# A triangular inverse built from blocks of 4 with half-width merges, and weight sums formed by an accumulating DMA

## The chip, the cores and the metric

The kernel runs on one core of one Trainium2 chip. The metric is the device time of one execution in microseconds; the time before is the median of three runs. A trace of one further execution shows what each engine did. The engines are named as the profile names them: PE (TensorE), PEld (its weight loads), DVE (VectorE), ACT (ScalarE), POOL (GpSimd), SP (the queue that issues most transfers).

## What is computed

One layer of a hybrid decoder over 512 tokens of width 2048, all in float32. The cut reference:

```python
h = rms_norm(x, norm_w)
proj = h @ w_in            # two branches (8 heads of 128 each), their gates
# branch A, per head, chunks of 64 tokens:
a_mat = where(strict, beta * (k @ k.T) * exp(cum_g[i] - cum_g[j]), 0)
sol   = triangular_solve(eye + a_mat, [v * beta, k * beta * exp(cum_g)], lower, unit_diagonal)
# ... chunk-by-chunk state recurrence with qk, q_dec, k_dec, g_last
# branch B, per head: block-sparse softmax attention (blocks of 256 keys)
y_gdn, y_moba = oa @ w_out_gdn, ob @ w_out_moba
merged = sigmoid(g_gdn) * y_gdn + sigmoid(g_moba) * y_moba
x = x + merged @ w_o
```

The triangular solve is done here through the explicit inverse of `eye + a_mat`, a 128x128 matrix for each of four groups of 128 tokens.

## The kernel before

**The head loop.** Eight heads follow one another, 117.7 us each. PE works through the input projection in windows: `win(n, k0, k1)` is the k steps k0 to k1 of a window, three 128x512 matmuls each (lines 740, 742, 744), and between these pieces stand the small products of branch A of head h and of branch B of head h-1. Every engine's program is written out by hand in one fixed order and paced by counted semaphores, so each small product stands some k steps behind the one whose result it needs. `four(ps, lhsT, rhs)` (L769) is four 128x128 products for the four token groups; the trace shows eight matmul instructions for it, each with its own weight load. `turn(ps, src)` (L774) is four transposes, four instructions.

**The inverse.** DVE forms the exponent of the decay matrix with one instruction for each token group (L1692), ACT takes the exponential, POOL masks it (L644). `kk` multiplies the products of the keys by it, `UT` and `LT` turn the result twice. From the blocks of 16 on the diagonal (`Ud`, `Ld`), `n1` to `n4` build the inverse of these blocks by repeated squaring. `ma(h, k)` and `mb(h, k)` then merge blocks: ma takes the product of the masked lower part with the inverse so far, and the inverse's transpose; mb multiplies the two and DVE adds the result. Levels 0 and 1 (to blocks of 32 and 64) work on full 128x128 matrices, level 2 on 64x64 corners. `vTs` turns v, and DVE scales it to `vb`, which ma(h, 0) waits for.

**The quads.** After the heads come ten quads 0 to 9 with 224 units of 12 matmuls (L1161, L1163, L1165), 2.74 us a unit when nothing waits. A quad multiplies four blocks of weights in seven products, named P11, PS1, PS2, P12, PS4, PS3, P22. ACT copies a unit's operand to `ring_hi` (L1520, `op_hi`), DVE forms `ring_lo` (L2117, `op_lo`), and PE uses both. Quads 0 to 3, 8 and 9 have four units a product; quads 4 to 7 have two (their weights are w_out_gdn and w_out_moba). PS1 takes the weights A21 - A11 and PS2 that sum plus A22. With four units POOL adds A22 by an accumulating DMA on the operand in place (`add_22`, L691), issued when op_lo has read PS1's operand. With two units DVE does it (`form_t2`, L2219), from a copy of A22 in the upper half of slot A. POOL's queue also stores the blocks (`finish_block`, L699, L702) and in quads 6 and 7 accumulates them from memory (L710).

ACT's order around a product is: `op_hi` of PS2's two units, then the copies of P11's result out of PSUM (L1561, `copy_out`), which PE waits for before it writes the same banks for PS2.

**The last head** has no next projection, and DVE puts ten `own_step` instructions (L2077, 128x2048) between its other work.

Of the kernel before, what the change touches and what calls it, by code (L numbers as in the profile page):

```python
# [13 lines left out]
P = 128  # L14
# [66 lines left out]
def t_base(q):  # L81
    return sum((3 if ku(b) == 4 else 4) * ku(b) for b in range(q))
# [6 lines left out]
def t2_formed(q, j):  # L89
    return t_base(q) + ku(q) + j + 1  # L90


def t4_formed(q, j):
    return t_base(q) + (1 if ku(q) == 4 else 2) * ku(q) + j + 1


def t3_formed(q, j):
    return t_base(q) + (2 if ku(q) == 4 else 3) * ku(q) + j + 1


def added(q):
    return 16 * (sum(ku(b) == 4 for b in range(q)) + 1)
# [20 lines left out]
def place(n):  # L123
# [41 lines left out]

(HC_G, HC_CG, HC_B, HC_NB, HC_NBE, HC_KD, HC_GL) = range(7)
# [11 lines left out]
 hcol cgrow_mm cg_rows cg_arg cg_eg cg_dt cg_dts  # L178
 conv clampd sig silu sqd sq_hi sq_lo ss_mm rn_ln rn norm
 kT_mm kdec kk_mm kkd qk_mm qkd qdec UT_mm Ln LT_mm Ud Ld X1 L32m L64m  # L180
 n1_mm L2 U2 n2_mm X2 L4 U4 n3_mm X4 L8 n4_mm X8 ma_mm Y XT mb_mm X
# [10 lines left out]
def hybrid_layer(nc, x, norm_w, w_in, gdn_conv_w, gdn_a_log, gdn_dt_bias, gdn_norm_w, moba_q_norm_w,  # L192
# [8 lines left out]
    cg_dram = nc.dram_tensor("decay_rows", (H, T), F32, kind="Internal").ap()  # L201
# [5 lines left out]
    with ctx:  # L207
# [41 lines left out]
        cg_rows = sg[:NT * H, 0, 1, 0:P]  # L249
# [29 lines left out]
        lm = [sb(f"lower{i}", [P, T], at=area) for i in range(3)]  # L279
# [27 lines left out]
        cgb = sb("decay_row", [P, T], at=area)  # L307
# [8 lines left out]
        Eg, L2, Yt = w2_, w2_, w2_  # L316
        dTs, L4 = w0_, w0_
        Up, U2, XTt = w1_, w1_, w1_
        Ud, U4, vn = w3_, w3_, w3_
        Ld, L8, o1 = w4_, w4_, w4_  # L320
        Ln = lm[0]
# [7 lines left out]
        def tile4h(t):  # L329
            return slice(t * P, t * P + P // 2), slice(t * P + P // 2, (t + 1) * P)  # L330

# [284 lines left out]
        def _(pool):  # L616
# [15 lines left out]
            def decay_row(h):  # L632

                pool.wait_ge(s["cg_eg"], h)
                pool.wait_ge(s["cg_arg"], 4 * h)
                pool.dma_start(cgb[:], cg_dram[bass.ds(h, 1), :].broadcast_to([P, T])).then_inc(s["cg_rows"], 16)

            def head(h, p):
# [3 lines left out]
                pool.wait_ge(s["cg_dt"], h + 1)  # L642
                pool.wait_ge(s["n3_mm"], h)
                pool.tensor_tensor(q4(dTs), q4(dT), over(plane(C_STRICT)), ALU.mult).then_inc(s["cg_dts"], 1)  # L644
# [7 lines left out]
                pool.wait_ge(s["Ln"], h + 1)  # L652
                pool.wait_ge(s["ma_mm"], 3 * h)
                pool.tensor_tensor(q4(lm[1]), q4(Ln), over(plane(C_L32)), ALU.mult).then_inc(s["L32m"], 1)
                pool.tensor_tensor(q4(lm[2]), q4(Ln), over(plane(C_L64)), ALU.mult).then_inc(s["L64m"], 1)
# [19 lines left out]
            pool.wait_ge(s["hc_set"], 2 + NHC + 1)  # L675
            for t in range(NT):
                pool.dma_start(cg_dram[:, tile4(t)], cg_rows[t * H:(t + 1) * H, :]).then_inc(s["cg_rows"], 16)
# [38 lines left out]
            for q in range(NQ):  # L716
                if q == W0:
                    finish_block(q - 1, 3)
                if ku(q) == 4:
                    add_22(q, 0)  # L720
                    add_22(q, 1)
                if q > 0 and q != W0:
                    finish_block(q - 1, 3)
                if ku(q) == 4:
                    add_22(q, 2)
                    add_22(q, 3)
                for i in range(3):
                    finish_block(q, i)
# [6 lines left out]
        def _(pe):  # L735
# [42 lines left out]
            def cgrow(h):  # L778
                pe.wait_ge(s["hcol"], h + 1)
                for t in range(NT):  # L780
                    mm = pe.matmul(G2[:, tile4(t)], hcol[:, HC_G, t:t + 1].broadcast_to([P, P]), triu,
                                   start=True, stop=True)
                mm.then_inc(s["cgrow_mm"], 1)
# [23 lines left out]
            def UT(h):  # L807
                pe.wait_ge(s["kkd"], h + 1)
                pe.wait_ge(s["kdec"], h + 1)
                turn(G0, Up).then_inc(s["UT_mm"], 1)  # L810

            def LT(h):
                pe.wait_ge(s["Ln"], h + 1)
                turn(G2, Ln).then_inc(s["LT_mm"], 1)

            def n1(h):
                pe.wait_ge(s["Ud"], h + 1)
                pe.wait_ge(s["Ld"], h + 1)
                pe.wait_ge(s["qkd"], h + 1)
                four(G0, Ud, Ld)  # L820
                four(G1, Ld, Ud).then_inc(s["n1_mm"], 1)

            def n2(h):
                pe.wait_ge(s["L2"], h + 1)
                pe.wait_ge(s["U2"], h + 1)
                pe.wait_ge(s["X1"], h + 1)
                four(G0, U2, L2)
                four(G1, L2, U2)
                four(G2, L2, xa).then_inc(s["n2_mm"], 1)

            def n3(h):
                pe.wait_ge(s["X2"], h + 1)
                pe.wait_ge(s["L4"], h + 1)
                pe.wait_ge(s["U4"], h + 1)
                four(G0, U4, L4)
                four(G2, L4, xb).then_inc(s["n3_mm"], 1)

            def n4(h):
                pe.wait_ge(s["X4"], h + 1)
                pe.wait_ge(s["L8"], h + 1)  # L840
                four(G2, L8, xa).then_inc(s["n4_mm"], 1)

            def vTs(h):
                pe.wait_ge(s["silu"], 3 * h + 3)
                pe.wait_ge(s["U4"], h + 1)
                turn(G1, cv["gv"]).then_inc(s["vT_mm"], 1)

            def ma(h, k):
                src = (xb, xa, xb)[k]
                if k == 0:  # L850
                    pe.wait_ge(s["X8"], h + 1)
                    pe.wait_ge(s["L8"], h + 1)
                    pe.wait_ge(s["vb"], h + 1)
                elif k == 1:
                    pe.wait_ge(s["X"], 3 * h + k)
                if k < 2:
                    pe.wait_ge((s["L32m"], s["L64m"])[k], h + 1)
                    four(G0, lm[k + 1], src)
                    mm = turn(G1, src)
                else:  # L860
                    for t in range(NT):
                        a, b = tile4h(t)
                        pe.matmul(G0[:P // 2, b], Ln[P // 2:, a], src[P // 2:, b], start=True, stop=True)
                    for t in range(NT):
                        a, b = tile4h(t)
                        mm = pe.transpose(G1[:P // 2, a], src[:P // 2, a], ident[:P // 2, :P // 2])
                mm.then_inc(s["ma_mm"], 1)

            def mb(h, k):
                if k < 2:  # L870
                    pe.wait_ge(s["Y"], 3 * h + k + 1)
                    pe.wait_ge(s["XT"], 3 * h + k + 1)
                    mm = four(G2, XTt, Yt)
                else:
                    for t in range(NT):
                        a, b = tile4h(t)
                        mm = pe.matmul(G2[:P // 2, b], XTt[:P // 2, a], Yt[:P // 2, b], start=True, stop=True)
# [8 lines left out]
            def vnew(h, t):  # L886
                if t == 0:
                    pe.wait_ge(s["vb"], h + 1)
                    pe.wait_ge(s["X"], 3 * h + 3)
                else:  # L890
                    pe.wait_ge(s["vbk"], 3 * h + t)
                pe.matmul(G1[:, :P], xb[:, tile4(t)], vb[:, tile4(t)], start=True, stop=True).then_inc(s["vn_mm"], 1)
# [57 lines left out]
            def head(h, p):  # L950
# [21 lines left out]
                else:  # L972
# [6 lines left out]
                    pe.transpose(A2[:NT * H, P:2 * P], ba[:, 1].rearrange("p t h -> p (t h)"), ident[:])\  # L979
# [7 lines left out]
                UT(h)  # L987
                win(2, 12, 14)
                ss(h, 1)
                win(2, 14, 15)  # L990
                LT(h)
                win(2, 15, 16)
                win(3, 0, 1)
                qk(h)
                win(3, 1, 4)
                n1(h)
                win(3, 4, 7)
                n2(h)
                win(3, 7, 10)
                n3(h)  # L1000
                win(3, 10, 13)
                n4(h)
                win(3, 13, 16)
                vTs(h)
                win(4, 0, 2)
# [1347 lines left out]
```

## Time and profile before

| what | value |
|---|---|
| median of 3 runs | 1641.9 us (1641.84, 1641.90, 1643.56) |
| the profiled execution, its own time | 1643.3 us |
| its span, first to last instruction | 1641.8 us |
| PE busy | 1592.5 us (97%), 7858 matmul instructions |
| PEld busy | 1316.3 us (80%) |
| DVE busy | 1092.7 us (67%) |
| ACT busy | 790.1 us (48%) |
| POOL busy | 158.3 us (10%) |
| granted PE clock, share of full | 0.994 |

The times of the rows are in us from the span's start. A busy PE is not a PE at its peak: matmuls overlap, so what an instruction costs is read from the distance between starts, not from its own length.

### The profile page before, as it was taken

The numbers are of one execution on the slowest core, as the hardware profiler recorded it, in microseconds if no ns is written. First come the engines' busy times: TensorE is split into PE (matmuls) and PEld (weight loads), VectorE is DVE, ScalarE is ACT, GpSimd is POOL, SyncE is SP. The second block draws the span as 40 slices with busy tenths as digits, with TensorE's granted clock in tenths as the row PEclk, the third lists the DMA queues.
The fourth block names the chain that finished last, engine by engine and source line by source line (L and its number), as shares of the span: only waits on it lengthen the run. The fifth ranks groups of instructions, "written<-read, shape, count | busy, mean of one in ns | idle before, by whom it ended". The sixth has DMA issues, their size and how long they took to land.

```text
span 1641.8 us, 20823 instructions
## 1 busy us (share of the span) xinstructions
PE 1592.5 (97%) x7858; PEld 1316.3 (80%) x7858; DVE 1092.7 (67%) x1320; ACT 790.1 (48%) x1048; POOL 158.3 (10%) x154
## 2 busy tenths in 40 slices
PE   6999999999999999999999999999999999999997
PEld 5888888887887887887887887888888778777885
DVE  5745745645646646556568758867677999888863
ACT  5434534435434444335335346556465845447442
POOL 4101001001001000010011011011010000001011
PEclk9999999999999999999999999999999999999999
DMA  8304314223223233133143337576566556775653
GB/s 261 78 26 115 84 38 129 57 76 90 77 57 99 73 77 96 51 89 83 51 113 101 137 136 210 192 192 220 140 189 187 196 196 209 202 217 112 196 116 52
DMA packets 192379, 206.19 MB, mean 126 GB/s; under 512 B 7491, under 2 KB 139846, under 8 KB 190726
## 3 DMA queue, kind: packets, MB, share of 16 engines
q1 hardware_dynamic: 176470, 161.69, 33.2%
q0 software_dynamic: 15856, 43.80, 11.2%
q8 instruction: 33, 0.54, 0.1%
q14 instruction: 20, 0.16, 0.0%
HBM read 180.28 MB, written 29.38 MB: 128 GB/s over the span
## 4 chain that ended last, share of the span: by engine, by line
PE 81%; issue 6%; DVE 5%; DMA 5%; ACT 2%; POOL 1%; SPq 0%; ACTq 0%; POOLq 0%; DVEq 0%
PE bank L740 14%; PE bank L744 14%; PE bank L742 14%; PE bank L1161 8%; PE bank L1163 8%; PE bank L1165 8%; PE bank L769 6%; DMA e_block<-branch_a 2%; PE bank L774 1%; DVE ring_lo L2117 1%; PE bank L930 1%; PE bank L946 1%; DMA operands<-branch_a 1%; ACT ring_hi L1520 1%; PE bank L940 1%
## 5 line engine op out<-in xcount | busy, mean ns | idle before, releaser
L740 PE MATMUL bank<-h_hi_r,w_hi 128*128 128x512 f32 x1008 | 421.5, 418 | 0.0
L744 PE MATMUL bank<-h_hi_r,w_raw_r 128*128 128x512 f32 x1008 | 396.9, 394 | 0.0
L742 PE MATMUL bank<-h_lo_r,w_hi 128*128 128x512 f32 x1008 | 394.1, 391 | 0.0
L2117 DVE TENSOR_TENSOR ring_lo<-operands,ring_hi 128x1024 fp32r<-128x1024 f32 x224 | 271.8, 1221 | 117.8 <-ACT ring_hi L1520 116.8
L1520 ACT ACTIVATE ring_hi<-operands 128x1024 fp32r<-128x1024 f32 x224 | 235.5, 1059 | 230.0 <-PE bank L1165 174.4
L744 PEld LDWEIGHTS bank<-h_hi_r,w_raw_r 128*128 128x128 f32 x1008 | 189.1, 188 | 43.0
L742 PEld LDWEIGHTS bank<-h_lo_r,w_hi 128*128 128x128 f32 x1008 | 190.3, 189 | 35.6 <-issue 1.7
L740 PEld LDWEIGHTS bank<-h_hi_r,w_hi 128*128 128x128 f32 x1008 | 189.9, 188 | 35.8 <-issue 1.7
L1161 PE MATMUL bank<-ring_hi,h_hi_r 128*128 128x512 f32 x480 | 190.6, 397 | 3.1 <-issue 3.1
L1163 PE MATMUL bank<-ring_lo,h_hi_r 128*128 128x512 f32 x480 | 189.4, 395 | 0.0
L1674 DVE TENSOR_TENSOR w_raw_r<-w_raw,w_hi 128x2048 fp32r<-128x2048 f32 x64 | 146.7, 2292 | 45.9 <-ACT w_hi L1219 44.7
L1165 PE MATMUL bank<-ring_hi,h_lo_r 128*128 128x512 f32 x416 | 162.4, 390 | 0.0
L1165 PE MATMUL bank<-ring_hi,sums_r 128*128 128x512 f32 x384 | 150.1, 391 | 0.0
L1161 PE MATMUL bank<-ring_hi,sums_r 128*128 128x512 f32 x320 | 126.3, 395 | 7.6 <-DVE ring_lo L2117 4.3
L1163 PE MATMUL bank<-ring_lo,sums_r 128*128 128x512 f32 x320 | 125.1, 391 | 0.0
L1219 ACT ACTIVATE w_hi<-w_raw 128x2048 fp32r<-128x2048 f32 x64 | 122.2, 1909 | 0.0
L1161 PEld LDWEIGHTS bank<-ring_hi,h_hi_r 128*128 128x128 f32 x480 | 90.4, 188 | 24.5 <-issue 4.1
L1163 PEld LDWEIGHTS bank<-ring_lo,h_hi_r 128*128 128x128 f32 x480 | 90.7, 189 | 18.5 <-issue 0.2
L1165 PEld LDWEIGHTS bank<-ring_hi,h_lo_r 128*128 128x128 f32 x416 | 78.4, 188 | 17.3
L1165 PEld LDWEIGHTS bank<-ring_hi,sums_r 128*128 128x128 f32 x384 | 72.5, 189 | 15.6
L1161 PEld LDWEIGHTS bank<-ring_hi,sums_r 128*128 128x128 f32 x320 | 60.4, 189 | 22.5 <-issue 7.2
L1163 PEld LDWEIGHTS bank<-ring_lo,sums_r 128*128 128x128 f32 x320 | 60.5, 189 | 12.3
(324 smaller groups left out, 2179.4 us busy)
## 6 DMA issues: line engine op xcount, KB each, us to landing
w_raw<-in_w_in_dram SPq DMA_DIRECT2D x64, 1024.0 KB, 6.0
operands<-in_w_in_dram SPq DMA_DIRECT2D x64, 512.0 KB, 4.7
operands<-in_w_o_dram SPq DMA_DIRECT2D x32, 512.0 KB, 4.9
operands<-in_w_in_dram POOLq DMA_DIRECT2D x16, 512.0 KB, 8.7
gates<-e_block POOLq DMA_DIRECT2D x16, 512.0 KB, 5.3
operands<-in_w_out_gdn_dram SPq DMA_DIRECT2D x16, 512.0 KB, 4.0
operands<-gates SPq DMA_DIRECT2D x16, 512.0 KB, 5.2
operands<-in_w_out_moba_dram SPq DMA_DIRECT2D x16, 512.0 KB, 4.6
```

What stands on the lines that cost most here:

```text
L740: pe.matmul(PJ[slot % 2][:], w_hi[slot % 2][:, c], h_hi[:, k, :], start=(k == 0), stop=False, skip_group_check=True)
L742: pe.matmul(PJ[slot % 2][:], w_hi[slot % 2][:, c], h_lo[:, k, :], start=False, stop=False, skip_group_check=True)
L744: mm = pe.matmul(PJ[slot % 2][:], w_lo[slot][:, c], h_hi[:, k, :], start=False, stop=(k == KT - 1), skip_group_check=True)
L769: mm = pe.matmul(ps[:, tile4(t)], lhsT[:, tile4(t)], rhs[:, tile4(t)], start=True, stop=True)
L774: mm = pe.transpose(ps[:, tile4(t)], src[:, tile4(t)], ident[:])
L1161: pe.matmul(ps[:], a_hi, ring_hi[:, n % RINGS, c], start=(FRESH[p] and k == 0), stop=False, skip_group_check=True)
L1163: pe.matmul(ps[:], a_hi, ring_lo[:, n % RINGS, c], start=False, stop=False, skip_group_check=True)
L1165: mm = pe.matmul(ps[:], a_lo, ring_hi[:, n % RINGS, c], start=False, stop=(k == kn - 1), skip_group_check=True)
L1219: act.activation(w_hi[slot % 2][:], raw[slot][:], ACT.Copy).then_inc(s["hi_ready"], 1)
L1520: act.activation(ring_hi[:, n % RINGS, :], operand(q, p, j), ACT.Copy).then_inc(s["op_hi"], 1)
L1674: dve.tensor_tensor(w_lo[slot][:], raw[slot][:], w_hi[slot % 2][:].bitcast(F32), ALU.subtract)\
L2117: dve.tensor_tensor(ring_lo[:, n % RINGS, :], operand(q, p, j), ring_hi[:, n % RINGS, :].bitcast(F32), ALU.subtract).then_inc(s["op_lo"], 1)
```

## The change

**The inverse.** The squaring now stops at blocks of 4 (n1 and n2, one `four` each), and four levels of merges go from blocks of 4 to 64, then the unchanged level of 64x64 corners. In a merge from blocks of b only the rows and columns that change are touched: the matrix has m = 128 - b rows, and only every second block of columns moves, 64 of 128. The masked product is formed after PE, by DVE, which multiplies the 64 columns by a mask of pairs.

**Both orientations of the decay.** Instead of turning the product twice, the kernel forms the upper matrix (`dTb`) and the lower one (`dL`, `dLm`) of decay, beta and mask ahead of the product. The rows -beta are loaded beside the decay rows by the same transfer, now 128x1024. Three DVE instructions of 128x512 take the place of the four of 128x128, ACT gets a third exponential, POOL four products instead of three.

**The quads.** `form_t2` is gone; `add_22` runs for every quad.

```diff
@@ cgrow on DVE
-                for t in range(NT):
-                    dve.scalar_tensor_tensor(dT[:, tile4(t)], row[:, tile4(t)], hcol[:, HC_CG, t:t + 1],
-                                             plane(C_DMASK), ALU.subtract, ALU.add).then_inc(s["cg_arg"], 1)
+                dve.tensor_tensor(q4(dL), q4(row), hcb(HC_CG), ALU.subtract).then_inc(s["cg_arg"], 1)
+                dve.wait_ge(s["cg_arg"], 3 * h + 1)
+                dve.tensor_tensor(q4(dT), q4(dL), over(plane(C_DMASK)), ALU.add).then_inc(s["cg_arg"], 1)
+                dve.tensor_tensor(q4(dL), q4(dL), over(plane(C_CMASK)), ALU.subtract).then_inc(s["cg_arg"], 1)
@@ POOL, called at the start of each head
+            def decay_parts(h):
+                pool.wait_ge(s["cg_dl"], h + 1)
+                pool.tensor_tensor(q4(dL), q4(dL), hcb(HC_NB), ALU.mult).then_inc(s["cg_dts"], 1)
...
+                pool.tensor_tensor(q4(dTb), q4(dT), over(masked4), ALU.mult).then_inc(s["cg_dts"], 1)
...
+                pool.tensor_tensor(q4(dLm), q4(dL), over(masked4), ALU.mult).then_inc(s["cg_dts"], 1)
...
+                pool.tensor_tensor(dTb[:], dTb[:], nb_row, ALU.mult).then_inc(s["cg_dts"], 1)
@@ merges on PE
+                    m = P - b
+                    for t in range(NT):
+                        pe.matmul(G0[:m, t * PAIRED:(t + 1) * PAIRED], Ln[:, t * P:t * P + m],
+                                  half_tile(xa, t, b, 1), start=True, stop=True)
+                    for t in range(NT):
+                        mm = pe.transpose(G1[:m, t * P:t * P + m], xa[:m, t * P:t * P + m], ident[:m, :m])
...
+                    m = P - LEVELS[k]
+                    for t in range(NT):
+                        mm = pe.matmul(G2[:m, t * PAIRED:(t + 1) * PAIRED], XTt[:m, t * P:t * P + m],
+                                       Yt[:m, t * PAIRED:(t + 1) * PAIRED], start=True, stop=True)
@@ the end of the chain on PE
+                win(4, 10, 12)
                 vTs(h)
...
+                win(4, 12, 13)
+                pe.wait_ge(s["X"], NL * h + NL - 1)
+                pe.wait_ge(s["vb"], h + 1)
                 win(4, 13, 14)
+                ma(h, 4)
@@ POOL, quads
             for q in range(NQ):
...
-                if ku(q) == 4:
-                    add_22(q, 0)
-                    add_22(q, 1)
+                add_22(q, 0)
+                add_22(q, 1)
@@ DVE, quads
-            def form_t2(q, j):
...
-                dve.tensor_tensor(ops[:, SLOT_A, j, :], ops[:, SLOT_A, j, :], ops[:, SLOT_A, 2 + j, :], ALU.add)\
-                    .then_inc(s["t_formed"], 1)
```

In the first head the rows come straight from PE: `cgrow` there gets four more products (eight instructions), a second transpose and a copy, and DVE builds the masks before it (`level_masks`, nine instructions).

The order of DVE at the start of a head in the loop, before and then after. `w_raw_r` is the split of the next window's weights, `cst` holds the masks, and the rows of `bank` and `softmax_stats` are the attention of head h-1.

```order
L1674 TENSOR_TENSOR w_raw_r<-w_raw,w_hi 128x2048
L1687 ISA
L1689 REGISTER_ALU
L1692 SCALAR_TENSOR_TENSOR decayT<-decay_row,hcol,cst 128x128 x4
L1872 ISA
L1873 TENSOR_TENSOR bank<-bank,cst 128x128
```

```order
L1685 TENSOR_TENSOR w_raw_r<-w_raw,w_hi 128x2048
L1698 ISA
L1700 REGISTER_ALU
L1701 TENSOR_TENSOR lower<-decay_rows,hcol 128x512
L1702 ISA
L1703 TENSOR_TENSOR decayT<-lower,cst 128x512
L1704 TENSOR_TENSOR lower<-lower,cst 128x512
L1875 ISA
L1876 TENSOR_TENSOR bank<-bank,cst 128x128
```

Three instructions over all 512 columns now stand ahead of the first instruction of the softmax, where one group of four short ones stood.

POOL at the same place of the loop, before and then after: the last row of each is the store of branch B.

```order
L636 DMA decay_row<-decay_rows 128x512
L642 REGISTER_ALU
L644 TENSOR_TENSOR work<-decayT,cst 128x512
L649 ISA
L649 DMA branch_outputs<-probs 128x512
```

```order
L656 DMA decay_rows<-decay_rows 128x1024
L660 REGISTER_ALU
L661 TENSOR_TENSOR lower<-lower,hcol 128x512
L665 TENSOR_TENSOR work<-decayT,cst 128x512
L667 REGISTER_ALU
L668 TENSOR_TENSOR lower<-lower,cst 128x512
L670 ISA
L671 REGISTER_ALU
L672 TENSOR_TENSOR work<-work,decay_rows 128x512
L683 ISA
L683 DMA branch_outputs<-probs 128x512
```

Four products now stand together at the start of the head; the two that stood later in the head (L654, L655 of before) are gone.

POOL's queue from the end of quad 3 to quad 5, before and then after: `gates` and `branch_a` rows are stores of finished blocks, the `operands` rows that read weights are accumulating transfers.

```order
L699 DMA gates<-e_block 128x1024 x4
L702 DMA branch_a<-operands 128x1024
L702 DMA branch_a<-e_block 128x1024 x3
L702 DMA branch_a<-operands 128x1024
```

```order
L721 DMA operands<-in_w_out_gdn_dram 128x2x512 x2
L729 DMA gates<-e_block 128x1024
L732 DMA branch_a<-operands 128x1024
L732 DMA branch_a<-e_block 128x1024 x2
L721 DMA operands<-in_w_out_gdn_dram 128x2x512 x2
```

Two accumulating transfers of 512 KB now stand in each of the quads 4 to 7, ahead of the store of the last block of the quad before.

## Rows read from the trace of the kernel before

**Rows 1.** The page: busy time of each engine, its share, its instructions.

```profile
PE 1592.5 (97%) x7858; PEld 1316.3 (80%) x7858; DVE 1092.7 (67%) x1320; ACT 790.1 (48%) x1048; POOL 158.3 (10%) x154
```

**Rows 2.** Timeline of PE in the fourth head: start, length, engine, line, out<-in, shapes.

```profile
423.60 0.60 PE L774 MATMUL bank<-ident,work 128*128 128x128 f32 x4
...
424.26 0.39 PE L742 MATMUL bank<-h_lo_r,w_hi 128*128 128x512 f32 x1
424.50 0.40 PE L744 MATMUL bank<-h_hi_r,w_raw_r 128*128 128x512 f32 x1
...
428.42 1.05 PE L769 MATMUL bank<-conv_gq,conv_gk 128*128 128x128 f32 x8
...
429.55 0.40 PE L742 MATMUL bank<-h_lo_r,w_hi 128*128 128x512 f32 x1
```

**Rows 3.** Timeline of PE in the first head: weights of 128 columns, 32 moving columns.

```profile
51.21 0.30 PE L1074 MATMUL bank<-mgt,cst 128*128 128x32 f32 x2
51.35 0.39 PE L1075 MATMUL bank<-mgt,ones_f 128*128 128x32 f32 x2
...
51.89 0.39 PE L742 MATMUL bank<-h_lo_r,w_hi 128*128 128x512 f32 x1
```

**Rows 4.** Timeline of PE, the corner level mb(h, 2), weights and moving 64 wide.

```profile
464.48 0.39 PE L744 MATMUL bank<-h_hi_r,w_raw_r 128*128 128x512 f32 x1
464.80 0.68 PE L877 MATMUL bank<-work 64*64 64x64 f32 x8
...
465.75 0.39 PE L742 MATMUL bank<-h_lo_r,w_hi 128*128 128x512 f32 x1
```

**Rows 5.** Timeline of DVE at the start of the head loop's fourth head.

```profile
388.52 2.29 DVE L1674 TENSOR_TENSOR w_raw_r<-w_raw,w_hi 128x2048 fp32r<-128x2048 f32 x1 [6.18 <-ACT w_hi L1219]
390.73 1.14 DVE L1692 SCALAR_TENSOR_TENSOR decayT<-decay_row,hcol,cst 128x128 f32<-128x128 f32 x4
391.78 0.29 DVE L1873 TENSOR_TENSOR bank<-bank,cst 128x128 f32<-128x128 f32 x1
...
393.93 0.29 DVE L1886 TENSOR_SCALAR bv<-bv,softmax_stats 128x128 f32<-128x128 f32 x1
```

**Rows 6.** PE at that place, then line 940 over the span: what its waits ended on.

```profile
394.27 0.33 PE L940 MATMUL bank<-ident,bv 128*128 128x128 f32 x1
...
  DVE bv L1886: 2.9, 7
```

**Rows 7.** Timelines of POOL and of DVE where both work at once.

```profile
473.69 1.80 POOL L664 TENSOR_TENSOR k_rope<-pt,cossin 128x512 f32<-128x512 f32 x1 [46.06 <-DVE pt L1852]
...
474.37 1.67 DVE L1859 TENSOR_TENSOR pt<-pt,cossin 64x512 f32<-64x512 f32 x1
```

**Rows 8.** Timelines of PE and of DVE around the turn of v.

```profile
446.90 0.60 PE L774 MATMUL bank<-ident,conv_gv 128*128 128x128 f32 x4
...
447.54 0.69 DVE L1784 TENSOR_TENSOR v_beta<-bank,hcol 128x512 f32<-128x512 f32 x1 [1.85 <-PE bank L774]
```

**Rows 9.** Timelines of DVE and of PE in the first head.

```profile
56.79 0.18 DVE L1679 COPY hcol<-hc 128x28 f32<-128x28 f32 x1
...
57.82 1.05 PE L781 MATMUL bank<-cst,hcol 128*128 128x128 f32 x8
```

**Rows 10.** Timelines of DVE, ACT and PE in quad 4, between PS1 and PS2.

```profile
1297.95 1.21 DVE L2117 TENSOR_TENSOR ring_lo<-operands,ring_hi 128x1024 fp32r<-128x1024 f32 x1
...
1301.01 1.22 DVE L2219 TENSOR_TENSOR operands<-operands 128x1024 f32<-128x1024 f32 x1
...
1302.32 1.06 ACT L1520 ACTIVATE ring_hi<-operands 128x1024 fp32r<-128x1024 f32 x1 [4.27 <-DVE operands L2219]
...
1306.41 1.07 ACT L1561 ACTIVATE operands<-bank 128x512 f32<-128x512 f32 x2
...
1307.53 0.80 PE L1161 MATMUL bank<-ring_hi,h_lo_r 128*128 128x512 f32 x1 [3.69 <-ACT operands L1561]
```

**Rows 11.** Line 691, the accumulating transfers of before: issue to landing.

```profile
DMA to landing us min/median/max: 5.7/8.6/10.6
```

More of the change, by code:

```diff
@@ L81, in t_base, with t4_formed, added @@
 def t_base(q):
-    return sum((3 if ku(b) == 4 else 4) * ku(b) for b in range(q))
+    return sum(3 * ku(b) for b in range(q))
 def t1_formed(q, j):
     return t_base(q) + j + 1
-def t2_formed(q, j):
+def t4_formed(q, j):
     return t_base(q) + ku(q) + j + 1
-def t4_formed(q, j):
-    return t_base(q) + (1 if ku(q) == 4 else 2) * ku(q) + j + 1
 def t3_formed(q, j):
-    return t_base(q) + (2 if ku(q) == 4 else 3) * ku(q) + j + 1
-def added(q):
-    return 16 * (sum(ku(b) == 4 for b in range(q)) + 1)
+    return t_base(q) + 2 * ku(q) + j + 1
+def added(q, j):
+    return 16 * sum(j < ku(b) for b in range(q + 1))
 def op_loads(q, j, slot, nth=0):
@@ L278, in hybrid_layer @@
         w0_ = sb("work0", [P, T], at=area)
-        lm = [sb(f"lower{i}", [P, T], at=area) for i in range(3)]
+        Ln, dL, dLm = [sb(f"lower{i}", [P, T], at=area) for i in range(3)]
         xa = sb("inv_a", [P, T], at=area)
@@ L314, in hybrid_layer @@
         cos, sin = cossin[:, 0, :], cossin[:, 1, :]
[L316 to L321, printed above, removed]
+        cg_row, nb_row = rows2[:, 0, :], rows2[:, 1, :]
+        Eg, Yt = w2_, w2_
+        dTb, L2 = w0_, w0_
+        XTt = w1_
+        Ud, vn = w3_, w3_
+        Ld, o1 = w4_, w4_
+        masked4 = plane(C_STRICT)
+        steps = plane(C_L64)
         probs = [bv, pr1]
@@ L330, in tile4h, with half_of, half_tile, compact @@
             return slice(t * P, t * P + P // 2), slice(t * P + P // 2, (t + 1) * P)
+        def half_of(ap, b, which):
+            return ap[:].rearrange("p (n s b) -> p n s b", s=2, b=b)[:, :, which, :]
+        def half_tile(ap, t, b, which):
+            return ap[:, tile4(t)].rearrange("p (n s b) -> p n s b", s=2, b=b)[:, :, which, :]
+        def compact(ap, rows):
+            return ap[:rows, :NT * PAIRED]
+        def paired(k):
+            at = plane((C_M16, C_L32)[k // 2])
+            return at[:, (k % 2) * PAIRED:(k % 2 + 1) * PAIRED]
         def corner(ap, half):
@@ L782, in cgrow @@
                                    start=True, stop=True)
+                for t in range(NT):
+                    mm = pe.matmul(G1[:, tile4(t)], hcol[:, HC_NB, t:t + 1].broadcast_to([P, P]), ident[:],
+                                   start=True, stop=True)
                 mm.then_inc(s["cgrow_mm"], 1)
@@ L856, in ma @@
[L856 to L859, printed above, removed]
+                    pe.wait_ge(s["X2"], h + 1)
+                    pe.wait_ge(s["qkd"], h + 1)
+                elif k < NL - 1:
+                    pe.wait_ge(s["X"], NL * h + k)
+                if k == NL - 1:
+                    for t in range(NT):
+                        i, j = tile4h(t)
+                        pe.matmul(G0[:P // 2, j], Ln[P // 2:, i], xa[P // 2:, j], start=True, stop=True)
+                    for t in range(NT):
+                        i, j = tile4h(t)
+                        mm = pe.transpose(G1[:P // 2, i], xa[:P // 2, i], ident[:P // 2, :P // 2])
```

336 lines of the change are left out of this document (156 added, 180 removed).

## The prediction

> **What bounds the kernel now.** I first read the page's shares: PE is busy for 97% of the span and DVE for 67% [rows 1]. The span is PE's, so time taken off PE comes off the span one for one, as long as nothing that PE waits for becomes later. Then I read PE's timeline for what a group of small products costs. The lengths overlap, so I take distances between starts: from a group's first instruction to the second window product behind it, less one ordinary distance of 0.24 (424.26 to 424.50). A `four` costs 1.13 - 0.24 = 0.89 us for its eight instructions, 0.111 each; a `turn` costs 0.66 - 0.24 = 0.42 for four, 0.105 each [rows 2]. Last I looked for the places where PE does wait. In the head loop that is one, in seven heads: the first transposes of the softmax (L940) start 0.05 us after DVE has scaled `bv`, and line 940 waited 2.9 us over 7 times, so each delay of DVE there is PE's [rows 5, 6]. After the heads it is the turn from PS1 to PS2 in the two-unit quads: PE stood 3.69 us in quad 4 [rows 10].
>
> **The inverse on PE.** Before, a head has 96 instructions of `four` at full width (n1 16, n2 24, n3 16, n4 8, and 8 in each ma and mb of levels 0 and 1) and 16 transposes (UT, LT and two levels): 96 x 0.111 + 16 x 0.105 = 12.34 us. After, there are 16 for n1 and n2 (1.78), 64 in four levels of merges, and 16 transposes. The corner level and `vTs` stay. The number of groups between window pieces stays at 13, so their edges cancel.
>
> What do the 64 cost, whose weights have m = 124, 120, 112 and 96 columns (113 on average, 0.883 of 128), and whose moving side has 64? Two things could set the distance: the weight load or the moving columns. The nearest row has weights of 128 columns and only 32 moving: four instructions cost 0.68 - 0.24 = 0.44, or 0.11 each, the same as with 128 moving [rows 3]. So a narrow moving side alone gains nothing, and the weights' columns decide. I take 0.111 x 0.883: 64 x 0.098 = 6.27, and for the transposes 16 x 0.105 x 0.883 = 1.48. The sum after is 9.53, a saving of 2.81 per head, **22.5 us** for eight. Bounds: if the distance does not fall with m at all, the 80 and 16 instructions cost 10.56, and 1.78 is saved per head (14.2 in all). If the moving side counted and the 64 cost half, the sum is 1.78 + 3.55 + 1.48 = 6.81, and 5.5 is saved per head (44). The corner level speaks for some caution: with both sides at 64 its eight instructions cost 1.27 - 0.48 = 0.79, hardly less than 0.89, though the group itself is 0.68 long instead of 1.05; what is gained inside is lost at the edges [rows 4, 2]. A line between 64 and 128 columns through these totals gives 0.87 for a group of eight, and a saving of about 2.0 per head (16). I stay with 22.5, since the new groups use more than half of the array's rows and columns, as the full ones do.
>
> **The start of each head on DVE.** Behind the split of the weights the four instructions of L1692 occupy DVE for 1.05 us (390.73 to 391.78) [rows 5]. Three of 128x512 with 0.69 each [rows 8] take their place. They follow one another at about 0.60, the length less the overlap of 0.09 that row 391.78 shows, and the second waits for the first's result, which costs the overlap once: 1.92 us. That is 0.87 later for everything behind, and `bv` ends this chain without slack [rows 6]. Seven heads: **+6.1 us**. Below, a third of it could go if the second does not wait fully (+4.5); the case above is a rival below.
>
> **Behind the chain: vb.** The wait for `vb` now stands one k step behind `vTs`. Before, `vb` was ready at 447.54 + 0.69 = 448.23, 1.33 us after the turn began at 446.90 [rows 8]. PE gets there after the turn and three window products, 0.42 + 3 x 0.23 = 1.12. I count 0.25 per head, 2.0 for eight. In the last head DVE carries an own step of 128x2048 between the steps of the chain, 2.29 long by the row of that shape [rows 5]; one stands ahead of the last merges, and one ahead of `vb`. I count 1.0 and 2.2 there. Together **+5.2 us** (0 to 8). In the chain itself I find no wait by laying the DVE and ACT steps of 0.6 to 0.7 between pieces of three k steps of 2.1 us.
>
> **The first head.** Nine short instructions of 0.18 or somewhat more (1.8 us) come ahead of `hcol`, which is ready 0.85 before PE needs it (56.97 against 57.82) [rows 9]: +0.95. Eight more products and a transpose: 0.89 + 0.1 = +1.0. And four products on POOL now lie beside DVE's convolution, where one lay before. An instruction of DVE that reads two tiles of SBUF stretches beside one of POOL, from 0.69 to 1.67 us [rows 7, 8], and the first transposes of k wait for the end of that row: +1.8. Sum **+3.7 us** (1 to 7). In the other heads the same blocking falls on `zmul` and on the second pair of softmax steps, which have over a microsecond to spare; I count nothing, and the rival prices it if this cover is gone.
>
> The Trainium skill, page "SBUF — State Buffer", section "Who interferes with whom", calls the port pair that DVE and GpSimd share "an exclusive lock". By that rule each of POOL's four products can hold up one such DVE instruction for its full length; the row of 1.67 us agrees.
>
> **The transfer of rows** is 128x1024 instead of 128x512. It is issued a head's beginning ahead of its use, so I count nothing.
>
> **The two-unit quads.** `form_t2` leaves DVE (eight times 1.2 us), and the operand of PS2 now comes by a transfer that can only be issued when op_lo of PS1 has read the old one. In quad 4 op_lo of PS1's second unit ends at 1297.95 + 1.21 = 1299.16, and without the form_t2 ahead of it at 1298.0 [rows 10]. From issue to landing such transfers took 5.7 to 10.6 us, 8.6 in the middle [rows 11]. For the second of two I take 6.9, between the shortest and the middle, since few other transfers run at this time: it lands at 1304.9, op_hi follows at 1305.0 instead of 1302.32. ACT's copies of P11's result are queued behind that op_hi, and PE waits for them (1307.53): everything shifts by 2.7 us [rows 10]. In quads 5 to 7 DVE and ACT have the same order and I expect 2 to 2.5 each; in quads 6 and 7 POOL's queue also has the accumulating block transfers of before ahead of them. Back comes some of DVE's 2.4 us per quad at the next P11. Sum **+9.5 us**, with bounds 0 and 14.
>
> The Trainium skill, page "DMA: Bandwidth & Descriptors", section "Anatomy of one DMA — SWDGE (gpsimd) path", gives about 2.0 us plus the bytes at 436 GB/s, an estimate of 3.2 us for 512 KB. By that the transfer would land before op_hi needs it and this term would be nothing; the rows of this trace say 5.7 at least, so the trace disagrees.
>
> **The sum:** -22.5 + 6.1 + 5.2 + 3.7 + 9.5 = +2.0 us. The trace's own execution took 1643.3 us (span 1641.8), so 1645.3 against it. The median of the runs is 1.4 lower, 1641.9; the prediction for it is **1644**. A measurement of this kernel can tell about 0.2% (3.3 us) from no change, so this is no measurable change.
>
> **The rivals.**
> 1. *The merges pay by their moving columns*: saving 44 instead of 22.5, the time 1622. Against it stand the rows with 32 moving columns [rows 3]; for it, that the corner group is so much shorter inside [rows 4].
> 2. *The accumulating transfers are hidden*: they land within 4.3 us of op_lo, or op_hi of PS2 is not what the copies wait for. Then the term of 9.5 falls away, and the time is 1634; at the shortest landing seen, 5.7, about half remains and it is 1639.
> 3. *POOL gets in first at the start of a head* (the other side). By the lengths above, DVE reaches the clamp of `zclamp` about when ACT's third exponential ends and POOL may start. If POOL's first product starts ahead of the clamp or the scaling that stands before `bv`, DVE's next is 1.0 to 1.2 us longer, as L1859 was [rows 7]: seven times 1.2 is 8.4, the time 1652. It decides if that exponential ends before DVE reaches the clamp.
> 4. *Narrow groups cost as much as full ones*: a saving of 14.2, the time 1652; with edges like those of the corner level [rows 4] 16, and 1650.
>
> **How the numbers follow.** The forecast has 0.40, with its own range 1638 to 1650 from the bounds of `vb`, the first head and the quads. Rival 1 has 0.12, rival 2 0.18, rival 3 0.12, rival 4 0.13, and several smaller losses at once 0.05. Faster by over 0.2% (below 1638.6): 0.12 + 0.18 + 0.10 of the forecast's case = 0.40. Slower (above 1645.2): 0.12 + 0.13 + 0.05 + 0.08 = 0.38. Between: 0.22. The range 1628 to 1654 leaves out rival 1 and the far ends of rivals 3 and 4.
>
> **What would show it.** In the changed kernel's timeline the groups of m columns lie 0.098 apart (0.111 under rival 4, about 0.056 under rival 1). Line 940's transposes start 0.87 later behind the split than before. PE waits about 0.25 at `vb` in each head. Accumulating transfers in quads 4 to 7 land 6 to 8 us after their issue, and ACT's op_hi of PS2 waits on them, not on DVE. I am wrong if a group in the chain waits in every head for a mask or an addition on DVE, since each such wait counts eight times.

## The result, and the profile after

The changed kernel takes 1670.7 us (median of 4 runs, 1670.1 to 1672.2) against 1641.9 before: the ratio is 1.0177, 95% interval 1.0163 to 1.0191, so it is slower by 1.8%, or 29 us. The forecast was 1644 with a range of 1628 to 1654. The profiled execution has a span of 1668.6 us against 1641.8.

The page's busy times, which answer to [rows 1]:

```profile
PE 1586.6 (95%) x7739; PEld 1306.8 (78%) x7739; DVE 1091.7 (65%) x1314; ACT 790.0 (47%) x1049; POOL 176.3 (11%) x170
```

PE has less to do and yet the span is 27 us longer. PE's waits up to the end of the head stage, as engine, line, what it waited for, us in total, times, the longest:

```profile
PE bank L956 <- DVE bv L1889: 12.7, 7, 1.8
PE bank L803 <- DVE conv_gk L1738: 4.8, 1, 4.8
PE bank L892 <- DVE work L1789: 4.2, 1, 4.2
PE bank L769 <- DVE v_beta L1775: 1.2, 7, 0.2
```

and from 1300 to 1520 us, the quads with two units and the first unit behind them:

```profile
PE bank L1178 <- ACT operands L1572: 14.4, 3, 6.1
PE bank L1194 <- ACT h_lo L1587: 7.0, 1, 7.0
PE bank L1194 <- DMA e_block<-branch_a: 4.2, 2, 2.4
PE bank L1178 <- issue: 3.1, 2, 2.0
PE bank L1194 <- DMA operands<-branch_a: 0.5, 1, 0.5
```

The same stretch of before (1290 to 1490) had 6.4 + 5.7 + 3.7 + 0.3 = 16.1 us of waits; now it is 29.2. In the quads ahead of it the waits fell from 4.3 to 3.2 us.

There is a second loss that no list of waits shows. The windows view gives the granted clock (the last but two of the numbers). Two pairs of stretches, the first of each behind a wait of PE (6.08 us up to 1317.26, 1.83 us up to 516.51):

```profile
1317.00:1322.00 5.00, 4.74 (x11) 3.77 (x12) 3.81 (x4) 4.96 (x7) 0.12 (x1) 0.50 0.29 117
1323.00:1325.00 2.00, 2.00 (x10) 1.66 (x9) 2.00 (x2) 1.75 (x2) 0.00 (x0) 1.00 0.21 81
```

```profile
517.00:520.00 3.00, 3.00 (x8) 2.19 (x7) 2.48 (x6) 0.82 (x3) 2.28 (x2) 0.50 0.00 0
520.00:521.00 1.00, 1.00 (x5) 0.78 (x4) 0.00 (x0) 0.00 (x0) 0.00 (x0) 0.80 0.00 0
```

At 0.50 the clock is 1.2 instead of 2.4 GHz, and the timeline shows what this does: matmuls of 128x512 start 0.43 us apart (1317.86, 1318.28, 1318.71) instead of 0.23. PE is "busy" meanwhile, so the time is counted as work. There are ten such stretches behind waits now, with 37.7 us of PE's busy time in them; before there were three, with 9.5 us. Half of it is lost: 18.8 against 4.7 us, that is **14 us more**: some 8 in the head stage (the first head, two of the middle ones, the last) and 6 in the quads. (The trace of before has a fourth stretch at the start of the program, 17 to 20 us, and the trace of changed has none there; it is not in the account.)

The head stage gives the cost of one stretch without any estimate. PE stands the same 1.83 us in each of these heads, but the half clock follows only the second row:

```profile
399.54 0.33 PE L956 MATMUL bank<-ident,bv 128*128 128x128 f32 x1 [1.83 <-DVE bv L1889]
516.51 0.33 PE L956 MATMUL bank<-ident,bv 128*128 128x128 f32 x1 [1.83 <-DVE bv L1889]
635.02 0.33 PE L956 MATMUL bank<-ident,bv 128*128 128x128 f32 x1 [1.82 <-DVE bv L1889]
```

From the first row to the second it is 116.97 us, from the second to the third 118.51: one stretch costs 1.54 us.

So the account of the two traces is, in us:

| part | forecast | measured |
|---|---|---|
| inverse on PE | -22.5 | -22 |
| first transposes of seven heads | +6.1 | +12.7 (the first line of the list above) |
| first head | +3.7 | +5.6 (waits 5.5, the new products 1.0, less 0.9 of waits before) |
| vb and the last head | +5.2 | +5.1 (1.2 at vb, 4.2 at mb(3), less 0.3 before) |
| waits in the two-unit quads | +9.5 | +13.1 (29.2 less 16.1) |
| waits in the quads ahead of them | not in the sum | -1.1 (3.2 less 4.3) |
| clock behind waits | not in the sum | +14.1 |
| sum | +2.0 | +27.5 (span: +26.8) |

### The profile page after: what moved, and what is told of

Same layout as the page of the kernel before. It is cut to its first block, busy times and chain, and to the rows that moved or that the text cites. A ratio compares the mean times of both kernels' runs of the same rounds, so it can differ in the third digit from the quotient of the medians.

```text
span 1668.6 us, 20685 instructions
## 1 busy us (share of the span) xinstructions
PE 1586.6 (95%) x7739; PEld 1306.8 (78%) x7739; DVE 1091.7 (65%) x1314; ACT 790.0 (47%) x1049; POOL 176.3 (11%) x170
## 3 DMA queue, kind: packets, MB, share of 16 engines
q0 software_dynamic: 18480, 49.85, 12.7%
## 4 chain that ended last, share of the span: by engine, by line
PE 74%; DVE 9%; issue 7%; DMA 5%; ACT 3%; POOL 1%; ACTq 0%; SPq 0%; DVEq 0%; POOLq 0%
PE bank L769 13%; PE bank L773 12%; PE bank L771 12%; PE bank L1178 8%; PE bank L1180 8%; PE bank L1182 8%; DVE ring_lo L2143 2%; PE bank L798 2%; PE bank L892 1%; PE bank L874 1%; DMA operands<-in_w_out_moba_dram 1%; PE bank L962 1%; DMA operands<-in_w_out_gdn_dram 1%; DMA e_block<-branch_a 1%; ACT ring_hi L1531 1%
```

## Experiments

The ratios are to the kernel before, run on the same chip. "Changed" is the kernel with the whole change, ratio 1.0177. The chip is not the same for all experiments (before takes 1638.8 to 1641.9 us), so an expectation in us is compared as a ratio to 1641.9.

**e1: POOL starts behind the scaling of bv.**

```diff
-            def decay_parts(h):
+            def decay_parts(h, p):
+                if p is not None:
+                    pool.wait_ge(s["s_norm"], 4 * p + 1)
                 pool.wait_ge(s["cg_dl"], h + 1)
```

> The changed kernel, but in the seven later heads POOL starts its four products only when DVE has scaled bv for the first transposes (L1889). Theory (POOL blocks DVE): L1889 falls from 1.25 to about 0.29 us, PE's wait at the first transposes from 1.83 to about 0.9, so 7 x 0.96 = 6.7 us go, and the two stretches of half clock behind such waits (517 and 752 us) go with them, 3 us more: about 1661. Rival (only the three long DVE instructions count, POOL is nothing): no change, 1670 to 1671. If POOL then blocks the later scalings so that their transposes wait instead, the gain is less than 6.

The ratio is 1.0146 (1.0129 to 1.0163), 5 us less than changed. The theory's 1661 is a ratio of 1.0116, below the interval, and the rival's 1670 is just above it, so the time lies between the two and the trace has to decide. First the changed kernel's timelines of DVE, POOL and PE in the fourth head (start, length, engine, line), which answer to [rows 5, 6]:

```profile
394.15 0.69 DVE L1701 TENSOR_TENSOR lower<-decay_rows,hcol 128x512 f32<-128x512 f32 x1
394.87 0.69 DVE L1703 TENSOR_TENSOR decayT<-lower,cst 128x512 f32<-128x512 f32 x1
395.48 0.69 DVE L1704 TENSOR_TENSOR lower<-lower,cst 128x512 f32<-128x512 f32 x1
396.08 0.29 DVE L1876 TENSOR_TENSOR bank<-bank,cst 128x128 f32<-128x128 f32 x1
...
398.23 1.25 DVE L1889 TENSOR_SCALAR bv<-bv,softmax_stats 128x128 f32<-128x128 f32 x1
...
396.91 1.26 POOL L661 TENSOR_TENSOR lower<-lower,hcol 128x512 f32<-128x512 f32 x1 [11.66 <-ACT lower L1282]
398.14 1.26 POOL L665 TENSOR_TENSOR work<-decayT,cst 128x512 f32<-128x512 f32 x1
...
399.54 0.33 PE L956 MATMUL bank<-ident,bv 128*128 128x128 f32 x1 [1.83 <-DVE bv L1889]
```

And the same place in e1:

```profile
396.57 0.29 DVE L1891 TENSOR_SCALAR bv<-bv,softmax_stats 128x128 f32<-128x128 f32 x1
...
397.02 1.04 POOL L663 TENSOR_TENSOR lower<-lower,hcol 128x512 f32<-128x512 f32 x1 [13.44 <-DVE bv L1891]
```

The three exponents take 396.08 - 394.15 = 1.93 us, as forecast (1.92). The scaling of bv then begins 0.09 us behind POOL's second product and takes 1.25 instead of 0.29; in e1 it takes 0.29. PE's wait at L956 is 0.9 instead of 1.8 in every head. So POOL's product is what lengthens the scaling, and the rival (POOL is nothing) is excluded by the trace. Both stretches of half clock in the middle of the head stage are gone too, but that can't be credited to this edit: in e3 the seven waits of 1.8 us stand as in changed, and no half clock follows any of them. Up to the first transposes of the last head e1 is 9.3 us ahead of changed (861.2 against 870.5 us), and some 3 of them are these two stretches. In the last head a later scaling is held up instead (an eighth wait of 0.9 us at this line); at its end the trace of e1 is 7.1 us shorter, on a chip on which before is 3 us faster.

The Trainium skill, page "SBUF — State Buffer", section "Who interferes with whom", says that `tensor_scalar` can enter a mode that takes the shared ports too, and that "whoever issues first gets the shared pair for the whole instruction". These rows agree. The rows of the first head (under e7) don't: there the DVE instruction began at 65.40 us, 0.8 ahead of POOL's first product, and yet it ended only behind the fourth. The sum of the prediction had used the part of the rule on two SBUF inputs alone.

**e2: the exponents behind the scaling of bv.** DVE's `cgrow` moves, and ACT's two exponentials follow the first copy of pt.

```diff
-                    cgrow(h)
                     softmax_max(p, 0)
                     zclamp(p, 1)
                     softmax_max(p, 1)
                     softmax_norm(p, 0)
+                    cgrow(h)
```

> The changed kernel, but DVE forms the three exponents of the decay behind the first scaling of the softmax instead of ahead of it, and ACT takes the two exponentials behind the first copy of pt; POOL's products start some 3 us later. Theory (the first transposes of each head wait for this chain): the wait of 1.8 us in seven heads goes altogether, 13 us and some 3 us of half clock: about 1655. Rival (the DVE and POOL work is only moved in front of the next scaling, and the second or third transposes wait instead): 1662 to 1670.

The ratio is 1.0111 (1.0094 to 1.0128), 11 us less than changed. The theory's 1655 is 1.0080 and lies below the interval; the upper expectation begins at 1.0122, inside it. The gain is smaller than the theory said, though its mechanism shows. PE's waits from 80 to 870 us in e2:

```profile
PE bank L956 <- DVE probs L1894: 2.0, 7, 0.3
PE bank L769 <- DVE v_beta L1780: 1.2, 7, 0.2
PE bank L956 <- DVE bv L1894: 0.9, 1, 0.9
```

Of the 12.7 us at the first transposes none is left in its place; 2.0 have moved to the second ones (POOL now holds up the scaling of probs, 1.50 us long), and one wait of 0.9 comes in the last head. A head in the middle of the loop takes 115.4 us against 117.7 before and 117.0 in changed. So a middle head now gains 2.3 us over before, where it gained 0.7 in changed.

**e3: the second weight sum on DVE again** (`form_t2` and its counts as before, `add_22` for four units alone).

```diff
-                add_22(q, 0)
-                add_22(q, 1)
+                if ku(q) == 4:
+                    add_22(q, 0)
+                    add_22(q, 1)
```

> The changed kernel with the second weight sum of the two-unit quads on DVE again, as before; the inverse stays new. Theory (the accumulating transfers land 6 to 10 us after op_lo, 15 in quad 7, and the copies behind op_hi with them): quads 4 to 7 give back their 20.7 us, 1650. Rival (half of that loss comes from the head stage, which ends 7 us later and shifts the quads against their transfers): 1660.

The ratio is 1.0068 (1.0051 to 1.0086), 18 us less than changed, of 20.7 expected. The theory's 1650 (1.0049) lies just below the interval, the rival's 1660 (1.0110) well above: nearly all of the part's cost comes back with this edit. By the traces of before and changed it is 13.1 us of waits and some 6 of half clock.

**e4: the accumulating transfers alone**, on the kernel before (the reverse edit).

> The kernel before with this one part of the change alone: the second weight sum by accumulating transfer in all quads. Theory: 1642 + 20.7 = about 1662, with PE's waits of 4 to 7 us at PS2 of quads 4 to 7 and half a clock behind them. Rival (the transfers cost only in company of the new head stage): 1642 to 1650.

The ratio is 1.0151 (1.0134 to 1.0168), +25 us, more than the theory's 21 and far from the rival. This part is a loss by itself. The rows that say why are those of changed, POOL, ACT and PE in quad 4, which answer to [rows 10]:

```profile
1303.42 1.22 POOL L721 DMA_DIRECT2D operands<-in_w_out_gdn_dram  x1 [2.90 <-DVE ring_lo L2143]
1305.69 1.21 POOL L721 DMA_DIRECT2D operands<-in_w_out_gdn_dram  x1 [1.05 <-DVE ring_lo L2143]
...
1309.52 1.06 ACT L1531 ACTIVATE ring_hi<-operands 128x1024 fp32r<-128x1024 f32 x1 [6.03 <-DMA operands<-in_w_out_gdn_dram]
1312.06 1.06 ACT L1531 ACTIVATE ring_hi<-operands 128x1024 fp32r<-128x1024 f32 x1 [1.48 <-DMA operands<-in_w_out_gdn_dram]
...
1316.14 1.07 ACT L1572 ACTIVATE operands<-bank 128x512 f32<-128x512 f32 x2
...
1317.26 0.80 PE L1178 MATMUL bank<-ring_hi,h_lo_r 128*128 128x512 f32 x1 [6.08 <-ACT operands L1572]
```

This is the mechanism of the prediction: op_hi waits for the landing, ACT's copies stand behind op_hi, PE behind the copies. PE's wait of 3.69 grew by 2.4, forecast 2.7. The later quads are worse. Line 721 over 1300 to 1460, then quad 7, POOL, ACT and PE:

```profile
DMA to landing us min/median/max: 5.8/7.7/11.8
```

```profile
1446.04 0.85 POOL L740 DMA_DIRECT2D e_block<-branch_a  x1 [8.20 <-DVE e_block L2167]
1446.91 2.42 POOL L721 DMA_DIRECT2D operands<-in_w_out_moba_dram  x2
...
1456.93 1.06 ACT L1531 ACTIVATE ring_hi<-operands 128x1024 fp32r<-128x1024 f32 x1 [14.82 <-DMA operands<-in_w_out_moba_dram]
1457.90 1.07 ACT L1587 ACTIVATE h_lo<-bank 128x512 f32<-128x512 f32 x2
...
1459.11 1.30 PE L1194 MATMUL bank<-ident,e_block 128*128 128x128 f32 x5 [6.99 <-ACT h_lo L1587]
```

op_lo of PS1 had ended at 1443.4, but the two transfers stand behind a block transfer (L740) in POOL's queue, which itself was issued only at 1446.04 when the one before it had landed and DVE was done. They are issued at 1446.9, run beside it and land 10 and 12 us later, where those of quad 4 took 6. That the block transfer beside them is what makes them slow was not tried. ACT waits 14.8 us, and PE 7.0.

**e5: both edits, e2 and e3.**

> The changed kernel with both edits of before at once: the exponents of the decay behind the first scaling of the softmax, and the second weight sum of the two-unit quads on DVE. Theory (two separate losses of the same change): they add, ratio to before 1.0177 - 0.0066 - 0.0109 = 1.000, about 1642 on the chip of the first timing. Rival (each takes away the same idle time or the same half clock): 1.004 or more, 1648.

The ratio is 0.9979 (0.9967 to 0.9992). The two losses add, and the rival (1.004) is excluded; the ratio is even a little below what adding gives (1.0002), and the kernel is now 0.2% faster than before.

**e6: the own steps of the last head.** On e5, own steps 8, 9 and 10 stand behind the chain of merges: 8 behind `zmul`, 9 and 10 behind the split of window 6.

```diff
-                if h is last:
-                    own_step(8)
                 split(n + 5, 1)
                 ma(h, 3)
                 zclamp(h, 0)
-                if h is last:
-                    own_step(9)
                 mb(h, 3)
-                if h is last:
-                    own_step(10)
                 vTs(h)
                 zmul(h, 0)
+                if h is last:
+                    own_step(8)
                 ma(h, 4)
                 mb(h, 4)
                 split(n + 6, 2)
+                if h is last:
+                    own_step(9)
+                    own_step(10)
```

> As the kernel with both edits, and in the last head the own steps 8 to 10 of DVE, which stand ahead of the mask of the last full merge and wait there for a store of row_sums, come behind the chain. Theory (PE's wait of 4.2 us at mb(3) of the last head is this one): the wait goes and with it the half clock behind it, 5 to 6 us less, ratio 0.996. Rival (the last head's DVE is the bound there and the wait moves to the next product): no change, 1.000.

The ratio is 0.9961 (0.9946 to 0.9976), 3 us less than e5 instead of 5 to 6, and its interval overlaps that of e5, so the total alone decides nothing. The DVE rows of changed in the last head show the wait that the edit takes away, and PE's list of e6 (900 to 985 us) where it went:

```profile
930.27 2.29 DVE L2103 TENSOR_TENSOR sg<-h_hi_r 128x2048 f32<-128x2048 f32 x1 [3.41 <-DMA row_sums<-sg]
932.49 2.29 DVE L1685 TENSOR_TENSOR w_raw_r<-w_raw,w_hi 128x2048 fp32r<-128x2048 f32 x1
934.69 0.41 DVE L1789 TENSOR_TENSOR work<-bank,cst 96x256 f32<-96x256 f32 x1
```

```profile
PE bank L824 <- DVE pt_r L1859: 3.5, 1, 3.5
```

The mask of the last full merge (L1789) stood behind an own step that waited 3.4 us for a store, and behind a split. It is free now, but the two own steps behind the split hold up `pt_r`. The rival was right that the wait moves.

**e7: the first head's products on DVE, vTs one k step earlier**, on e6.

```diff
-                decay_parts(h)
+                if p is not None:
+                    decay_parts(h)
@@ DVE, head
                 kT(h)
+                if p is None:
+                    decay_parts(h)
                 silu(h, 1)
@@ PE, head
-                win(4, 10, 12)
+                win(4, 10, 11)
                 vTs(h)
-                win(4, 12, 13)
+                win(4, 11, 13)
```

> As the kernel before this one in the list, and in the first head DVE does the four products of the decay itself, after the turn of k, instead of POOL; and vTs stands one k step earlier. Theory (the third convolution instruction of 6.1 us is held up for as long as POOL's four products follow one another, and PE's wait of 4.8 us is its end): that instruction falls to 0.75, the wait at the turn of k to under 1 us, some of it comes back at n1; and the wait for vb, 0.2 in each head, goes: 4 to 7 us less, ratio 0.993. Rival (DVE is simply short of time in the first head): the wait is the same or moves to n1, 1 us or nothing.

The ratio is 0.9935 (0.9919 to 0.9952), as expected, 4 us less than e6, with intervals that still touch. The first head of changed, DVE and POOL (the third of three instructions in the first row took 6.1 us, against 0.75 each of the others), and then the same DVE row in e7:

```profile
63.83 7.66 DVE L1720 SCALAR_TENSOR_TENSOR conv_gq<-raw_gq,chan,conv_gq 128x512 f32<-128x512 f32 x3
...
66.20 1.07 POOL L661 TENSOR_TENSOR lower<-lower,hcol 128x512 f32<-128x512 f32 x1
67.20 1.30 POOL L665 TENSOR_TENSOR work<-decayT,cst 128x512 f32<-128x512 f32 x1
68.44 1.28 POOL L668 TENSOR_TENSOR lower<-lower,cst 128x512 f32<-128x512 f32 x1
69.66 1.27 POOL L672 TENSOR_TENSOR work<-work,decay_rows 128x512 f32<-128x512 f32 x1
```

```profile
63.87 2.33 DVE L1741 SCALAR_TENSOR_TENSOR conv_gq<-raw_gq,chan,conv_gq 128x512 f32<-128x512 f32 x3
```

With POOL's products away the three take 2.33 us together, so it was the products that held the third. The wait of 4.8 us at the turn of k is gone, 3.2 us are back at n1 (L804), more than the "some" that was expected, and none is left at vb, which is the second edit's doing.

**e8: the price of a small product**, for the distances between starts alone, on changed (one execution).

```diff
-                        pe.matmul(G0[:m, t * PAIRED:(t + 1) * PAIRED], Ln[:, t * P:t * P + m], half_tile(xa, t, b, 1), ...)
+                        if k in (0, 2):   # all 128 columns of weights, 64 moving
+                            pe.matmul(G0[:, t * PAIRED:(t + 1) * PAIRED], Ln[:, tile4(t)], half_tile(xa, t, b, 1), ...)
+                        else:             # m columns of weights, all 128 moving
+                            pe.matmul(G0[:m, tile4(t)], Ln[:, t * P:t * P + m], xa[:, tile4(t)], ...)
```

> The changed kernel with two sizes changed on PE, for the price alone: in ma of levels 0 and 2 all 128 columns of weights are loaded (64 moving), in ma of levels 1 and 3 the weights stay at m columns and all 128 columns move. The output is the same. Theory (the distance between starts is that of the slower of weight load and moving side): with 128 columns of weights 0.111 us at both levels instead of 0.108 and 0.098; with 120 and 96 columns and 128 moving 0.109 to 0.111 instead of 0.105 and 0.085. Rival 1 of the prediction (the moving side alone counts): 0.056 at levels 0 and 2. A pure weight bound: 0.105 and 0.085 at levels 1 and 3.

The first product of the last full merge (k = 3) in changed, and then those of the last two (k = 2 and k = 3) in e8 (PE's timeline):

```profile
456.74 0.81 PE L874 MATMUL bank<-inv_a,lower 128*96 128x64 f32 x8
```

```profile
452.41 1.00 PE L875 MATMUL bank<-inv_a,lower 128*128 128x64 f32 x8
...
458.59 1.03 PE L878 MATMUL bank<-inv_a,lower 128*96 128x128 f32 x8
```

Within the groups the starts lie 0.085 us apart for 96 columns of weights and 64 moving, 0.112 for 128 and 64, and 0.109 for 96 and 128. Both sides count, and the slower one sets the distance. Over the levels of changed the distances are 0.108, 0.105, 0.098 and 0.085 for 124, 120, 112 and 96 columns: proportional to the columns, as forecast.

**e9 and e10: where the own steps stand**, on e7. In e9 own step 8 stands behind `zclamp`, 9 behind `vTs`, 10 ahead of the split of window 6; in e10 all three are where changed has them.

> As the kernel with the first head on DVE, but the own steps 8 to 10 of the last head are spread: 8 behind the mask of the last full merge, 9 behind the scaling of v, 10 ahead of the split, where both 9 and 10 stood behind the split and held up pt_r (PE waited 3.6 us for it). Theory: that wait falls to about 1.3 us and the half clock behind it goes; the chain gets at most 1 us of waits: ratio to before 0.991 to 0.993, 1 to 3 us less than the 0.9935 of the other. Rival (the last head has too much DVE work there for any order): 0.9935 again.

> The same with the own steps where the changed kernel has them. Theory: PE's wait of 4.2 us at mb(3) of the last head is back and 3 to 4 us of half clock with it, ratio 0.996 to 0.997. Rival (moving them gained nothing, since the wait only went on to pt_r): 0.9935.

e9 has the ratio 0.9901 (0.9886 to 0.9916), 1624.6 us against 1640.1 of before on that chip: the fastest kernel of the study, 1.0% faster than before. e10 has 0.9952 (0.9938 to 0.9965), a little under the 0.996 to 0.997 of the theory, and PE's wait of 4.2 us at mb(3) is back in it. So the spread order is worth 0.5%, some 8 us, and that of e7 a third of it, within what the intervals can tell. PE's waits in e9 up to the end of the head stage:

```profile
PE bank L804 <- DVE work L1770: 3.2, 1, 3.2
PE bank L962 <- DVE probs L1910: 2.0, 7, 0.3
PE bank L962 <- DVE bv L1910: 0.9, 1, 0.9
PE bank L825 <- DVE pt_r L1868: 0.5, 1, 0.5
```

A head in the middle of the loop takes 114.95 us in e9 against 117.7 before. These 2.75 us are what the new inverse is worth per head, 22 for eight.

## Why the prediction was wrong

Point by point, by its steps.

- **The inverse on PE** was right in mechanism and size: -22.5 forecast, -22 by the distances measured and by the heads of e9; rival 1 (the moving side alone) fell with e8, rival 4 (flat, or lost at the edges) with the distances of changed.
- **The sum left out the clock.** This is the step that failed most. Every wait was priced one for one ("each delay of DVE there is PE's" in the head loop, "everything shifts by 2.7 us" in the quads); in the trace a wait of PE is often followed by matmuls at 0.43 instead of 0.23 us. It cost 14.1 of the 29 us. The rows to see it were in the trace of before, behind the waits that end at 1307.53 and 1339.73; the page's mean of 0.994 hid it, and so I took no price from it. The stretch of before behind the first of these waits:

```profile
1308.00:1310.00 2.00, 2.00 (x6) 1.52 (x6) 1.55 (x2) 2.00 (x3) 0.00 (x0) 0.50 0.58 238
```

- **The waits too were priced too low.** Without the clock the measured parts add up to +13.4 instead of +2.0, which gives 1655 us, just above the end of the range at 1654. The terms that were short follow.
- **"Seven heads: +6.1 us"** was mis-sized: 12.7. The 0.87 us of the three long instructions was exact (their terms as written add up to 1.89 us, not 1.92; 1.93 was measured). The other 0.97 is POOL's second product, which e1 takes away alone. That was rival 3, with its place ("the scaling that stands before `bv`") and nearly its price (1.0 to 1.2), and I gave it 0.12. It deserved more, since the lengths in the sum already put POOL's start ahead of the scaling. The 2.9 us over 7 times that I read as PE's waits in [rows 6] were those of the weight loads: PE's own list of before has no such entry. The same paragraph takes 3.69 us as PE's wait in the quads, where the list of before has 12 more (6.4 put down to issue, 5.7 to the accumulating block transfers).
- **"The first head: +3.7"** measured 5.6. I counted POOL's hold on DVE once, 1.0 us by the rows, and wrote 1.8 without a row for the rest; one DVE instruction was held for all four products of POOL, 6.1 us, and e7 shows it by taking them away.
- **vb and the last head**: 5.2 forecast and 5.1 measured, but by other parts, so the agreement is luck. vb cost 0.17 per head, and the 4.2 us came from own step 8 waiting for a store, a wait that the step did not name.
- **The two-unit quads: "+9.5 us"** of waits, 13.1 measured. Quad 4 was right (2.4 for 2.7). Quad 7 was too low: the transfers wait behind L740 in POOL's queue and then take 10 and 12 us; I had counted the queue, not so late a landing. With the clock behind these waits the part costs more: e3 gives back 18 us and e4 loses 25. Rival 2 (hidden) fell.

In all, the forecast had most of the mechanisms in hand and misjudged how long the waits are and what follows them. The clock term has chance in it: of the seven equal waits of 1.8 us in a run two were followed by the half clock in changed, one in e8, none in e3.

## What to carry to other kernels

Price a wait of the matmul engine with the clock that follows it: look at the granted clock behind each wait of the trace of before, and add the half-speed stretch to the wait. A product moved to POOL can cost DVE up to its length where DVE scales or combines tiles in SBUF at that time, so keep it away from the short chain in front of PE, and never put several in a row beside such a chain. An in-place sum by a transfer is cheap only where the product that needs it stands far enough behind: four units of 2.74 us here, against 5.7 to 10.6 us to landing, and not with two.

## What the runs showed of the hardware

- The granted clock fell to 0.50 (1.2 of 2.4 GHz) behind waits of PE and in changed it stayed there for 3 to 5 us after the wait ended. Counted over PE's waits of 0.6 us and more in all twelve traces, from the first head to 1600 us: behind 66 waits shorter than 1.7 us it never fell, behind 54 of 1.7 to 3 us it fell 17 times, behind 22 of 3 to 4 us 20 times, and behind 30 of 4 us and more always. The Trainium skill, page "TensorE: Matmul & The Clock Gate", Part 1, states the two levels and that activity releases the lower one; the rows agree. What decides among waits of the same length stays open.
- POOL and DVE did not take turns evenly: beside four POOL products in a row one DVE scaling of 128x128 took 1.25 us and ended just behind the second, while a convolution step of 128x512, which began 0.8 us ahead of the first, took 6.1 us and ended behind the fourth. What decides between the two was not tried.
- Of the small fp32 products' two sides, weights and moving columns, the slower sets the distance, 0.85 to 0.89 ns a column (0.112 us for 128 columns of weights, 0.085 for 96, 0.109 for 128 moving beside 96 of weights).
